# Six moves in the program of a two-block network: two waits of merge, x turned earlier, a gate batch and a gate placed elsewhere, the first norm's squares folded

## The chip, the cores and the metric

The kernel runs on one core of one Trainium2 chip, in one launch. The metric is the device time of a launch in microseconds. The core's engines each run their own program in order: TensorE (PE, matrix products into PSUM), VectorE (DVE), ScalarE (ACT), GpSimd (POOL), and SyncE (SP), which here only issues DMAs. They wait for one another by semaphores.

## The reference, cut to what matters

The network has 256 tokens and 1024 features, all in fp32. First block:

```
x += short_conv_mixer(rmsnorm(x));  x += conv_ffn(rmsnorm(x))
x += moba_attention(rmsnorm(x));    x += conv_ffn(rmsnorm(x));  x = rmsnorm(x)
```

Second block (`x = second_block(x)`), where `hybrid_mixer` has three branches, each under a gate, and `peer_ffn` picks 16 of 16384 experts per head and token:

```
def rmsnorm(x, g):        return x * rsqrt(mean(x*x, -1) + 1e-6) * g
def stick_breaking(q,k,v): z = q@k.T*scale; a = exp(logsig(z) + sum_behind(logsig(-z))); return a @ v
m = sig(g0)*(o_stick @ w_sb) + sig(g1)*(o_nsa @ w_nsa) + sig(g2)*(o_hgrn @ w_hgrn)
x = x + m @ w_out
peer: y = sum_e gate_e(token) * gelu(x @ u_e) * v_e      # gates from a top-k over sub-keys
x = x + y;  return rmsnorm(x)
```

## The kernel before, in words

**Layout.** Activations lie transposed: features on the 128 partitions, 256 tokens on the free axis; x is 8 tiles of 128x256. All weights come as one stream of chunks of 128x1024 (512 KB). A chunk goes through a ring of three slots: SyncE loads it (`stream_all`, L404), ScalarE rounds it to its high part (`split_hi`, L417), VectorE takes the rest as its low part (`split_lo`, L429), and TensorE multiplies. `exact` (L455 to L457) makes three products of every fp32 one: high by high, high by low, low by high. A chunk is thus 24 rows of 256 columns on TensorE, or 12 of 512 in the expert stage. `arrived` makes TensorE wait for the low part. `walk_act` and `walk_dve` are the splits of the chunk three places on, which ScalarE does once TensorE has finished the chunk that had the slot.

**Order.** It is written by hand: the block at the end of the kernel calls for each engine the stages one after the other, and helpers put the splits between a stage's own operations. Nothing is scheduled by a program. An instruction that waits holds back all that follows on its engine.

**The start** (`start_act`, `start_dve`, `gated_pe`). SyncE issues the parameter table (`par`, 128x356), the first chunk, x in two halves, and then the stream. TensorE multiplies the unnormed x (times its gains, split by L603 and L609), and the norm's factor is applied to the results. For the factor ScalarE squares x (L614), TensorE sums the squares over partitions with a matrix of ones (`sums_pe`, L545: 8 fp32 products, two records each), ScalarE takes the root (`root_act`, L618), VectorE the reciprocal (`recip_dve`, L643). `sc` is the first mixer: three input chunks per step, and from the third step on one output chunk. `fold_dve` adds 8 tiles of squares to 2, and is used in a later norm (`split_pe`).

**Joints.** Between stages `joint_act` and `joint_dve` add the result to x pair by pair of tiles (`residual_add_dve`, L695, as `pair_done` comes), split and square it, and TensorE sums the squares between the rows of the next chunk (`first_pe`, L545).

**Stick-breaking** (`stick_pe`, `stick_act`, `stick_dve`). Eight heads in phases: scores, sums behind (L1210 and L1211, a bank each for even and odd heads), values (L1219 to L1221). Of the 24 chunks of merge gates (`gate_pe`, `gate_act` L1191) the first eight are put between them. VectorE makes the log weights (L1301), and splits gate 6 after that of head 3.

**Merge** (`merge_pe`, `merge_act`, `merge_dve`). The 20 chunks of `BR`: 12 of the three branches, in banks 4 to 7 in turn, and 8 of the output product, (3, 0) to (3, 7). The gates go through a sigmoid (L1580) on ScalarE once all 24 are copied.

**The experts** (`peer_pe`, `peer_act`, `peer_dve`). 128 chunks up and 128 down. The map of gates is made in 32 batches of 8 tokens for each half of the experts: VectorE makes one-hot rows (L1884 to L1891, `hots`), TensorE multiplies them (L1910, 16 rows), VectorE applies the result to the experts' outputs (`take_gates`, L1900). ScalarE (L1970) and VectorE (L2009) split a gated output, and TensorE adds it into banks 0 to 3 (`down_tokens`, L506) on top of x, which `x_tokens_pe` (L497) has turned there by products with the identity. The batches of the second half run beside experts 0 to 63 down, two experts and a batch a step; expert 64 needs the last batch.

## Time and profile before

| | us |
|---|---|
| median of 3 runs | 1833.99 |
| the three runs | 1830.77, 1833.99, 1834.78 |
| profiled execution, its time | 1833.53 |
| its span | 1831.7 |
| TensorE busy (matmul) | 1782.5 (97%) |
| VectorE busy | 1377.0 (75%) |
| ScalarE busy | 874.6 (48%) |
| mean granted TensorE clock | 0.987 of full |
| DMA queue of SyncE, share of 16 engines | 47.1% |

The busy shares are means over very different stages. What a moved instruction is worth is read where it stands: in the timeline, which merges like instructions and says in brackets how long the engine was idle before them and who ended it. The chain that ended last is 81% TensorE, 14% VectorE, 3% ScalarE.

### The profile page before, as it was taken

To read this page: it belongs to the slowest core of one execution; us is meant where nothing else is said; L and a number is where in the kernel's file an instruction comes from. 1 tells how busy PE (TensorE), PEld (TensorE's weight loads), DVE (VectorE), ACT (ScalarE), POOL (GpSimd) and SP (SyncE) were. 2 spreads that over 40 slices of the span, in tenths; PEclk is the share of its full clock that TensorE was granted. 3 is DMA by queue.
4 is the path that set the end of the run, shared out by engine and by line. 5 is a ranking of instruction groups with operands and counts; after the bars stand their busy time and mean duration, and the time that the engine had idled before them with its cause. 6 is when DMAs were issued, how large, how long until landed. Compare 5 with 4: busy or idle time off the path is not lost.

```text
span 1831.7 us, 37775 instructions
## 1 busy us (share of the span) xinstructions
PE 1782.5 (97%) x13634; PEld 1674.5 (91%) x13634; DVE 1377.0 (75%) x2489; ACT 874.6 (48%) x1348; POOL 19.6 (1%) x40
## 2 busy tenths in 40 slices
PE   8999999999999999999999999999999999999998
PEld 8999999988999999988899999999999888878886
DVE  5788889855888877355767699977777689985665
ACT  4343335355343374565563645454444344444544
POOL 0000000010000000000100000000000000000000
PEclk9999999999999999899999999999999999999999
DMA  5545555432555546332235345554544455455553
GB/s 201 194 153 191 172 186 170 161 104 73 188 176 179 187 159 221 105 104 70 69 128 173 123 165 172 170 185 162 168 165 171 142 170 182 167 165 188 192 194 137
DMA packets 79997, 292.31 MB, mean 160 GB/s; under 512 B 8928, under 2 KB 9088, under 8 KB 79664
## 3 DMA queue, kind: packets, MB, share of 16 engines
q1 hardware_dynamic: 79200, 287.93, 47.1%
q0 software_dynamic: 720, 3.32, 0.5%
q8 instruction: 53, 0.87, 0.2%
q14 instruction: 24, 0.20, 0.0%
HBM read 290.16 MB, written 1.05 MB: 159 GB/s over the span
## 4 chain that ended last, share of the span: by engine, by line
PE 81%; DVE 14%; ACT 3%; issue 1%; DMA 1%; DVEq 0%; SPq 0%; ACTq 0%
PE ps L506 19%; PE ps L455 18%; PE ps L456 17%; PE ps L457 17%; DVE m L429 5%; PE ps L1910 2%; DVE m L1813 2%; DVE m L1809 1%; PE ps L461 1%; PE ps L545 1%; DVE m L1817 1%; PE ps L1070 1%; PE ps L1069 1%; ACT m L417 1%; ACT m L603 1%
## 5 line engine op out<-in xcount | busy, mean ns | idle before, releaser
L455 PE MATMUL ps<-m,m 128*128 128x256 f32 x3312 | 958.9, 290 | 23.0 <-DVE m L429 11.2
L456 PE MATMUL ps<-m,m 128*128 128x256 f32 x3312 | 941.5, 284 | 0.0
L457 PE MATMUL ps<-m,m 128*128 128x256 f32 x3312 | 941.0, 284 | 0.0
L429 DVE TENSOR_TENSOR m<-m,m 128x1024 fp32r<-128x1024 f32 x542 | 657.1, 1222 | 257.7 <-ACT m L417 250.8
L455 PEld LDWEIGHTS ps<-m,m 128*128 128x128 f32 x3312 | 638.8, 193 | 37.9 <-issue 24.4
L417 ACT ACTIVATE m<-m 128x1024 fp32r<-128x1024 f32 x542 | 565.4, 1050 | 170.4 <-PE ps L457 155.5
L456 PEld LDWEIGHTS ps<-m,m 128*128 128x128 f32 x3312 | 638.7, 193 | 1.2 <-issue 0.2
L457 PEld LDWEIGHTS ps<-m,m 128*128 128x128 f32 x3312 | 638.1, 193 | 0.0
L506 PE MATMUL ps<-m,m 128*128 128x512 f32 x1536 | 358.8, 393 | 2.0 <-DVE m L2009 2.0
L506 PEld LDWEIGHTS ps<-m,m 128*128 128x128 f32 x1536 | 287.0, 189 | 60.6 <-issue 2.1
L1970 ACT ACTIVATE m<-m 128x256 fp32r (+1 forms) x128 | 53.4, 418 | 202.6 <-PE ps L506 194.8
L1952 ACT ACTIVATE m<-ps 128x256 f32 (+1 forms) x128 | 49.4, 386 | 195.8 <-PE ps L457 195.7
L873 ACT ACTIVATE m<-m 128x256 f32<-128x256 f32 x44 | 18.4, 419 | 163.8 <-DVE m L830 163.8
L2009 DVE TENSOR_TENSOR m<-m,m 128x256 fp32r<-128x256 f32 x128 | 54.4, 426 | 52.0 <-ACT m L1970 50.4
L1891 DVE TENSOR_TENSOR m<-m,m 128x512 f16<-128x512 f16 x128 | 54.0, 422 | 7.5
L1900 DVE SCALAR_TENSOR_TENSOR m<-ps,m 128x512 f32 (+1 forms) x64 | 43.7, 683 | 2.2 <-PE ps L1910 2.2
L1887 DVE TENSOR_TENSOR m<-m,m 128x1024 f16<-128x1024 f16 x64 | 43.8, 685 | 0.0
L1910 PEld LDWEIGHTS ps<-m,m 128*128 128x128 f16 x1024 | 34.5, 97 | 9.7 <-issue 8.4
L828 DVE SCALAR_TENSOR_TENSOR m<-m,m,m 128x255 f32<-128x255 f32 x96 | 42.3, 478 | 0.3
L830 DVE SCALAR_TENSOR_TENSOR m<-m,m,m 128x254 f32<-128x254 f32 x96 | 42.2, 477 | 0.3
L1126 ACT ACTIVATE m<-m,m 128x128 f32<-128x128 f32 x64 | 28.5, 447 | 29.0 <-DVE m L1147 18.5
L1910 PE MATMUL ps<-m,m 128*128 128x64 f16 x1024 | 42.1, 194 | 0.0
(252 smaller groups left out, 1142.6 us busy)
## 6 DMA issues: line engine op xcount, KB each, us to landing
m<-stream SPq DMA_DIRECT2D x542, 512.0 KB, 3.3
m<-alibi_t POOLq DMA_DIRECT2D x1, 1536.0 KB, 11.4
m<-con SPq DMA_DIRECT2D x1, 1417.0 KB, 7.4
m<-xT SPq DMA_DIRECT2D x2, 512.0 KB, 8.2
y<-m SPq DMA_DIRECT2D x4, 256.0 KB, 2.6
m<-wcmpk POOLq DMA_DIRECT2D x1, 512.0 KB, 5.3
m<-wcmpv POOLq DMA_DIRECT2D x1, 512.0 KB, 5.5
m<-fin POOLq DMA_DIRECT2D x1, 512.0 KB, 4.3
```

The costliest lines, as they stand in the source:

```text
L417: nc.scalar.activation(w_hi[:, r, :], raw[:, r, :], ACT.Copy).then_inc(hi_done, 1)
L429: nc.vector.tensor_tensor(w_lo[:, r, :], raw[:, r, :], w_hi[:, r, :].bitcast(F32), ALU.subtract)\
L455: nc.tensor.matmul(out, lhs[0], rhs[0], start=start, stop=False, **kw)
L456: nc.tensor.matmul(out, lhs[0], rhs[1], start=False, stop=False, **kw)
L457: return nc.tensor.matmul(out, lhs[1], rhs[0], start=False, stop=stop, **kw)
L506: ins = nc.tensor.matmul(acc[:, 2 * c + h, :], lhs, rhs[:, slot, h * 512:h * 512 + 512], start=False, stop=last, skip_group_check=True)
L1887: nc.vector.tensor_tensor(hot_b, iota_b.unsqueeze(1).broadcast_to(sb_), pairs(idx[:, 1, tok]).broadcast_to(sb_), ALU.is_equal)
L1891: ins = nc.vector.tensor_tensor(hot_a[:, i], hot_a[:, 1], pairs(gate_part[:, i, tok]).broadcast_to(sa), ALU.mult)
L1910: ins = nc.tensor.matmul(out, hot_b[:, q // 2, :, q % 2], hot_a[:, i, q // 2, :, q % 2], start=i == 0, stop=i == 1)
L1952: nc.scalar.activation(emap[:, st.lin(1), :], ps[:, 4 + st.mod(2), 0:T], ACT.Gelu).then_inc(gelu_done, 1)
L1970: nc.scalar.activation(ez[st.mod(2)][0], emap[:, st.lin(1), :], ACT.Copy).then_inc(ez_hi, 1)
L2009: nc.vector.tensor_tensor(ez[p][1], emap[:, st.lin(a, b), :], ez[p][0].bitcast(F32), ALU.subtract)\
```

## The change

Six edits, independent of one another.

1. *Start.* The parameter table is loaded in two pieces: its first 8 columns by ScalarE, the rest by SyncE behind the second chunk of the stream. x comes in one DMA behind the first chunk; both engines wait for all of it. VectorE folds the squares to two tiles, and TensorE sums these (4 rows) after the third chunk of the mixer, where 16 rows stood after the second. The root goes behind the third `walk_act` of the first step, the reciprocal behind its third `walk_dve`.
2. *Stick.* Gate 6 follows the sixth sum behind, not the fourth.
3. *Merge's first wait.* The first two branch chunks do not wait for the 24th gate's copy.
4. *Merge's last wait.* VectorE does not wait for the last two output chunks.
5. *x turned.* The products with the identity stand ahead of the wait for the first gated expert.
6. *Last gate batch.* It stands between experts 62 and 63, and not behind 63. The loop over steps is one turn shorter, and its five last steps are written out.

```diff
@@ stream_all
+            if st.s == 1:
+                sp.dma_start(tabs[:, KD:NPAR], par[:, KD:NPAR]).then_inc(s_par, 16)
@@
+    def folded_pe(v, b):
+        for j in range(2):
+            ins = nc.tensor.matmul(ps[:, b, 0:T], ones[:, 0:P], v[:, j, :], start=j == 0, stop=j == 1)
+        ins.then_inc(sum_ready, 1)
@@ gated_pe
-                    if i == 0 and st.s == 0 and u == 1:
-                        for k in range(4):
-                            sums_pe(pe, 0, k)
+                    if i == 0 and st.s == 0 and u == 2:
+                        pe.wait_ge(sq_folded, 1)
+                        folded_pe(sq, 7)
@@ start_act
+        act.dma_start(tabs[:, 0:KD], par[:, 0:KD]).then_inc(s_gain, 16)
         split_hi(act, Step(0), 1, 0)
-        act.wait_ge(s_par, 16)
+        act.wait_ge(s_gain, 16)
+        act.wait_ge(s_x, 16)
         for k in range(4):
-            act.wait_ge(s_x[k // 2], 16)
             wide_hi_act(act, 0, k)
...
         split_hi(act, Step(2), 1, 0)
-        root_act(act, 0)
@@ start_dve
         split_lo(dve, Step(1), 1, 0)
+        dve.wait_ge(sq_part, 4)
+        fold_dve(dc, sq)
         split_lo(dve, Step(2), 1, 0)
+        dve.wait_ge(s_par, 16)
+
+    def first_factor_dve(dve, dc):
         recip_dve(dve, dc, 0)
         dc.link(nc.vector.tensor_tensor(rope_a, rstd, rstd, ALU.mult))
@@ sc_dve
-                if u == 1:
+                if st.s == 0 and u == 2:
+                    first_factor_dve(dve, dc)
+                if u == (2 if st.s == 0 else 1):
                     dve.wait_ge(c_copied, st.lin(1, 1))
@@ sc_act
             walk_act(act, st, *up_at("sc", 4, st.s, 2))
+            if st.s == 0:
+                root_act(act, 0)
@@ stick_pe
             sums_behind(j)
-            if j == 3:
+            if j == 5:
                 gate_pe(pe, 6)
@@ merge_pe
-            pe.wait_ge(gate_raw, 3 * KD)
+            if b >= 2:
+                pe.wait_ge(gate_raw, 3 * KD)
@@ merge_dve
-            if i == 3:
+            if i == 3 and m + 2 < KD:
                 dve.wait_ge(chunk_done, CH["br"] + e + 1)
-                if m + 2 < KD:
-                    merged_dve(dve, dc, m + 2)
+                merged_dve(dve, dc, m + 2)
@@ expert_down_pe
-        pe.wait_ge(z_ready, st.lin(a, b + ZB["peer"] + 1))
         n = a * st.s + b
         if n == 0:
             x_tokens_pe(pe)
+        pe.wait_ge(z_ready, st.lin(a, b + ZB["peer"] + 1))
@@ peer_pe
-        steps(pe, None, 0, NB, 6, third, first=2)
+        steps(pe, None, 0, NB - 1, 6, third, first=2)
+        expert_down_pe(pe, Step(HALF - 2), 1, 0)
+        gates_of_batch_pe(pe, 1, Step(NB - 1))
+        expert_down_pe(pe, Step(HALF - 1), 1, 0)
         steps(pe, None, HALF, NKEY - 1, 6, lambda st: expert_down_pe(pe, st, 1, 0))
@@ sync
-            sp.dma_start(tabs[:, :], par).then_inc(s_par, 16)
             sp.dma_start(raw[:, 0, :], stream[0, :, :]).then_inc(ring_full[0], 16)
-            for h in range(2):
-                sp.dma_start(x[:, 4 * h:4 * h + 4, :], xT[:, 4 * h:4 * h + 4, :]).then_inc(s_x[h], 16)
+            sp.dma_start(x[:, :, :], xT).then_inc(s_x, 16)
```

The later users of `sq_folded` in `split_pe` count one higher, as the start now uses it too.

VectorE at the start, in the kernel before. `m_2_51` is the low part of a chunk, `m_14_63` the reciprocal root, `m_19_68` its square, `m_20_69` and `m_18_67` the scaled products.

```order
L429 TENSOR_TENSOR m_2_51<-m_0_49,m_1_50 128x1024 [waits chunk_hi_ready] x2
L643 RECIPROCAL m_14_63<-m_13_62 128x256 [waits rms_ready]
L676 TENSOR_TENSOR m_19_68<-m_14_63 128x256 [waits dve_chain]
L429 TENSOR_TENSOR m_2_51<-m_0_49,m_1_50 128x1024 [waits chunk_hi_ready,dve_chain]
L429 TENSOR_TENSOR m_2_51<-m_0_49,m_1_50 128x1024 [waits chunk_hi_ready]
L892 TENSOR_TENSOR m_20_69<-m_21_70,m_19_68 128x256 [waits c_copied]
L893 TENSOR_TENSOR m_18_67<-ps,m_14_63 128x256
L429 TENSOR_TENSOR m_2_51<-m_0_49,m_1_50 128x1024 [waits chunk_hi_ready,dve_chain]
```

The same place in the changed kernel, where `m_42_91` are the squares.

```order
L432 TENSOR_TENSOR m_2_51<-m_0_49,m_1_50 128x1024 [waits chunk_hi_ready]
L713 TENSOR_TENSOR m_42_91<-m_42_91 128x1024 [waits square_ready]
L714 TENSOR_TENSOR m_42_91<-m_42_91 128x512 [waits dve_chain]
L432 TENSOR_TENSOR m_2_51<-m_0_49,m_1_50 128x1024 [waits chunk_hi_ready]
L432 TENSOR_TENSOR m_2_51<-m_0_49,m_1_50 128x1024 [waits chunk_hi_ready,params_loaded]
L432 TENSOR_TENSOR m_2_51<-m_0_49,m_1_50 128x1024 [waits chunk_hi_ready] x2
L651 RECIPROCAL m_14_63<-m_13_62 128x256 [waits rms_ready]
L689 TENSOR_TENSOR m_19_68<-m_14_63 128x256 [waits dve_chain]
L902 TENSOR_TENSOR m_20_69<-m_21_70,m_19_68 128x256 [waits c_copied,dve_chain]
L903 TENSOR_TENSOR m_18_67<-ps,m_14_63 128x256
```

The two folding sums have come in behind the second chunk's split, and the splits of the fourth to sixth chunk stand ahead of the reciprocal, where two stood behind it and one behind the scaled products.

TensorE in the stick stage, before. `m_57_106` are the heads' log terms, `m_4_53` and `m_5_54` the two parts of the activations, `m_1_50` and `m_2_51` those of the chunk.

```order
L1210 MATMUL ps<-m_57_106,m_15_64 128x384 [waits log_weight_ready,softplus_whole]
L1211 MATMUL ps<-m_57_106,m_9_58 128x128
L455 MATMUL ps<-m_4_53,m_1_50 128x256 [waits chunk_lo_ready0,merge_gate_copied]
L456 MATMUL ps<-m_5_54,m_1_50 128x256
L457 MATMUL ps<-m_4_53,m_2_51 128x256
```

And in the changed kernel.

```order
L1222 MATMUL ps<-m_57_106,m_15_64 128x384 [waits log_weight_ready,softplus_whole]
L1223 MATMUL ps<-m_57_106,m_9_58 128x128
L1222 MATMUL ps<-m_57_106,m_15_64 128x384 [waits log_weight_ready,softplus_whole]
L1223 MATMUL ps<-m_57_106,m_9_58 128x128
L1222 MATMUL ps<-m_57_106,m_15_64 128x384 [waits log_weight_ready,softplus_whole]
L1223 MATMUL ps<-m_57_106,m_9_58 128x128
L458 MATMUL ps<-m_4_53,m_1_50 128x256 [waits chunk_lo_ready0,merge_gate_copied]
L459 MATMUL ps<-m_5_54,m_1_50 128x256
```

Two more pairs of sums, heads 4 and 5, stand between head 3's and the gate.

TensorE in the step of experts 62 and 63, before. `m_6_55`, `m_7_56` and `m_95_144`, `m_96_145` are the two parts of even and odd gated experts, `m_94_143` and `m_93_142` the one-hot rows.

```order
L506 MATMUL ps<-m_1_50,m_95_144 128x512 [waits chunk_lo_ready0]
L506 MATMUL ps<-m_1_50,m_95_144 128x512
L506 MATMUL ps<-m_2_51,m_95_144 128x512 x2
L506 MATMUL ps<-m_1_50,m_96_145 128x512 x2
L506 MATMUL ps<-m_1_50,m_95_144 128x512 x2
L506 MATMUL ps<-m_2_51,m_95_144 128x512 x2
L506 MATMUL ps<-m_1_50,m_96_145 128x512 x2
L1904 REGISTER_ALU
L1910 MATMUL ps<-m_94_143,m_93_142 128x64 [waits gate_map_taken,one_hots_ready]
L1910 MATMUL ps<-m_94_143,m_93_142 128x64 x15
```

And in the changed kernel.

```order
L509 MATMUL ps<-m_1_50,m_6_55 128x512 x2
L509 MATMUL ps<-m_2_51,m_6_55 128x512 x2
L509 MATMUL ps<-m_1_50,m_7_56 128x512 x2
L1922 MATMUL ps<-m_94_143,m_93_142 128x64 [waits gate_map_taken,one_hots_ready]
L1922 MATMUL ps<-m_94_143,m_93_142 128x64 x15
L509 MATMUL ps<-m_1_50,m_95_144 128x512 [waits chunk_lo_ready0,z_ready]
L509 MATMUL ps<-m_1_50,m_95_144 128x512
```

The 16 rows of the batch now stand behind the even expert's rows and ahead of the odd one's.

## Rows read from the trace of the kernel before

**Rows 1.** The page, busy us, share of the span, instructions.

```profile
PE 1782.5 (97%) x13634; PEld 1674.5 (91%) x13634; DVE 1377.0 (75%) x2489; ACT 874.6 (48%) x1348; POOL 19.6 (1%) x40
```

**Rows 2.** Chain of waits, start: start us, us, what.

```profile
1.67 7.78 DMA m<-xT
...
12.39 0.21 PE ps L457
...
19.07 0.12 PE ps L455
```

**Rows 3.** The instructions that load x: their landings.

```profile
DMA to landing us min/median/max: 7.8/8.2/8.6
```

**Rows 4.** Timeline of the start: start us, us, instructions, idle before.

```profile
11.62 0.55 PE L455 MATMUL ps<-m,m 128*128 128x256 f32 x1 [4.21 <-DVE m L609]
...
19.63 3.61 PE L545 MATMUL ps<-m,m 128*128 128x256 f32 x16
...
23.79 1.75 DVE L643 RECIPROCAL m<-m 128x256 f32<-128x256 f32 x1 [5.71 <-ACT m L618]
...
27.31 0.39 PE L455 MATMUL ps<-m,m 128*128 128x256 f32 x1 [1.20 <-DVE m L429]
...
33.24 2.44 DVE L429 TENSOR_TENSOR m<-m,m 128x1024 fp32r<-128x1024 f32 x2
```

**Rows 5.** VectorE, lines of `fold_dve`, 640 to 700 us.

```profile
L700 DVE TENSOR_TENSOR m<-m 128x1024 f32<-128x1024 f32 x2 | 2.4, 1218 | 0.0
...
L701 DVE TENSOR_TENSOR m<-m 128x512 f32<-128x512 f32 x2 | 1.4, 692 | 0.1
```

**Rows 6.** Windows: length; busy PE, PEld, DVE, ACT, POOL; granted clock; DMA share, GB/s.

```profile
699.30:706.00 6.70, 6.70 (x33) 6.70 (x33) 5.86 (x4) 0.55 (x3) 0.00 (x0) 0.50 1.00 344
...
818.80:822.10 3.30, 3.30 (x15) 3.00 (x14) 0.00 (x0) 0.48 (x1) 0.00 (x0) 0.50 0.28 103
...
945.00:948.40 3.40, 3.40 (x19) 3.40 (x17) 2.83 (x3) 3.37 (x3) 0.00 (x0) 0.50 0.16 28
...
1006.50:1009.80 3.30, 2.90 (x9) 2.58 (x10) 3.30 (x8) 3.30 (x9) 0.00 (x0) 0.50 0.30 114
```

**Rows 7.** Timeline, stick stage.

```profile
817.17 0.36 PE L455 MATMUL ps<-m,m 128*128 128x256 f32 x1 [2.36 <-DVE m L429]
...
828.21 0.41 PE L1219 MATMUL ps<-m,m 128*128 128x64 f32 x2 [0.79 <-DVE m L1512]
```

**Rows 8.** Timeline, last gate and first branch chunks of merge.

```profile
944.54 0.38 PE L455 MATMUL ps<-m,m 128*128 128x256 f32 x1 [2.82 <-ACT m L1191]
...
945.45 1.28 ACT L1580 ACT_TABLE_LOAD   x1
...
946.74 1.91 ACT L1580 ACTIVATE m<-m 128x2048 f32<-128x2048 f32 x1
...
950.39 1.22 DVE L429 TENSOR_TENSOR m<-m,m 128x1024 fp32r<-128x1024 f32 x1
...
963.38 1.22 DVE L429 TENSOR_TENSOR m<-m,m 128x1024 fp32r<-128x1024 f32 x1
```

**Rows 9.** Timeline, end of merge; last row: the first joint.

```profile
1003.47 1.23 DVE L429 TENSOR_TENSOR m<-m,m 128x1024 fp32r<-128x1024 f32 x1 [5.06 <-PE ps L457]
...
1006.90 2.05 PE L545 MATMUL ps<-m,m 128*128 128x256 f32 x4 [3.52 <-ACT m L614]
...
111.25 1.10 PE L545 MATMUL ps<-m,m 128*128 128x256 f32 x4 [0.18 <-ACT m L614]
```

**Rows 10.** Timeline, before the first expert down.

```profile
1446.35 5.47 PE L497 MATMUL ps<-m,m 128*128 128x128 f32 x32 [3.69 <-DVE m L2009]
```

**Rows 11.** Timeline, around the last gate batch.

```profile
1639.03 5.71 PE L506 MATMUL ps<-m,m 128*128 128x512 f32 x24
...
1640.46 0.88 DVE L1891 TENSOR_TENSOR m<-m,m 128x512 f16<-128x512 f16 x2
...
1647.19 9.18 PE L506 MATMUL ps<-m,m 128*128 128x512 f32 x32 [1.95 <-DVE m L2009]
```

More of the change, by code:

```diff
@@ L313, in build @@
     y_sum, y_mean, y_r = (at(O_HH + 3 * D + 8 * i, 2) for i in range(3))
-    s_x = sem("x_first_half_loaded"), sem("x_second_half_loaded")
+    s_x = sem("x_loaded")
+    s_gain = sem("first_weights_loaded")
     s_par = sem("params_loaded")
@@ L664, in start_act @@
         split_hi(act, Step(2), 1, 0)
-        root_act(act, 0)
     def start_dve(dve, dc):
         split_lo(dve, Step(0), 1, 0)
-        dve.wait_ge(s_par, 16)
+        dve.wait_ge(s_gain, 16)
+        dve.wait_ge(s_x, 16)
         for k in range(4):
-            dve.wait_ge(s_x[k // 2], 16)
             wide_lo_dve(dve, 0, k)
         split_lo(dve, Step(1), 1, 0)
+        dve.wait_ge(sq_part, 4)
+        fold_dve(dc, sq)
         split_lo(dve, Step(2), 1, 0)
+        dve.wait_ge(s_par, 16)
+    def first_factor_dve(dve, dc):
         recip_dve(dve, dc, 0)
@@ L704, in split_pe @@
         g, c = TC["p_split"], CH["p_split"]
-        def folded(v, b):
-            for j in range(2):
-                ins = nc.tensor.matmul(ps[:, b, 0:T], ones[:, 0:P], v[:, j, :], start=j == 0, stop=j == 1)
-            ins.then_inc(sum_ready, 1)
         for n in range(16):
@@ L720, in split_pe @@
             if n == 3:
-                pe.wait_ge(sq_folded, 1)
-                folded(sq, 7)
+                pe.wait_ge(sq_folded, 2)
+                folded_pe(sq, 7)
             if n == 6:
-                pe.wait_ge(sq_folded, 2)
-                folded(sq2, 5)
+                pe.wait_ge(sq_folded, 3)
+                folded_pe(sq2, 5)
         gates_pe(pe)
```

## The prediction, made before the result was known

> **What bounds the kernel now.** I began with the page: TensorE is busy for 1782.5 of the 1831.7 us [rows 1]. The profiled execution took 1833.53 us, so 1.8 us lie outside its span. Nothing but TensorE time can pay, and there are two kinds of it: its 49 us of pauses, and its rows at the lower of its two clock levels. I then went through TensorE's timeline for every row that has an idle time in front of it, and through the windows for the granted clock. At 0.50 (1.2 GHz) a row of 256 columns follows the last by 0.21 us, at 1.00 (2.4 GHz) by 0.12 us [rows 2]. So 3.4 us at the lower level hold work for 1.9 us, and cost 1.5. It is also lower in three places that the diff does not touch; the longest, 6.7 us at 699, stands for them [rows 6]. Its lower stretches at 818.8, 945.0 and 1006.5 [rows 6] each begin within 1.7 us of a pause of 2.4 to 3.5 us, and all three pauses are ones that the diff touches [rows 7 to 9]. So are the pauses of 3.69 us at 1446.35 and of 1.95 us at 1647.19 [rows 10, 11]. The change is therefore worth what these five stretches and the start are worth, each read by itself.
>
> **The start.** Before: x is issued at 1.67 us, its first half lands 7.78 us later, the second at most 8.6 us after its own issue [rows 2, 3], so at 10.7. From the first landing to the first weight row at 11.62 are 2.2 us of ScalarE and VectorE. Now the parameter table (178 KB) no longer stands ahead of the weights and x, and both engines wait for all of x. The table's place is worth between 0 and 1.1 us: x whole lands between 9.6 and 10.7. I take 9.9 (the queue had data to move in all of the time it would save, but the engines did not move it evenly), so the first weight row comes at 12.0, 0.4 later, and costs 0.2 us net because that time is at the lower clock. The small DMA of eight columns of the table, now issued by ScalarE, hides in the 7 us before x.
> The sums of squares: 16 rows in 3.47 us (19.63 until 23.1) become 4 rows, 0.87 us; this saves 2.6 us [rows 4]. VectorE pays for it with a fold of 1.22 + 0.69 us [rows 5]. It falls where VectorE idles before the third chunk's low part. Squares end near 16.3, the fold at 18.2, the low part at 19.4; TensorE, without the sums, wants that chunk at 19.8. Covered, with 0.3 us to spare.
> The pause of 1.20 us at 27.31 ends on VectorE's split of the fourth chunk [rows 4], which stood behind the root and the reciprocal (1.75 us at 23.79). Now the three splits go ahead of the reciprocal, and the pause goes. But something is late next. ScalarE comes to the root's table load only after the sixth chunk's high part (23.8); the load is 1.28 us [rows 8], so the root runs at 25.1, the reciprocal at 25.6, 1.85 us later than before. Without the three splits, which took 3.5 us of VectorE, the seventh chunk's split moves from 33.24 [rows 4] to 33.24 + 1.85 - 3.5 = 31.6 and ends at 32.85. TensorE, 3.6 us ahead, wants it at 32.2: a new pause of about 0.7 us. Net: 2.6 + 1.2 - 0.2 - 0.7 = 2.9 us. Bounds: 1.0 (x at 10.7 and the fold not covered), 4.5 (the clock rises earlier and the pause stays out).
> The table load was followed by its activation 0.01 us after its end, at 946.74 [rows 8]. The Trainium skill (ScalarE: Activation LUTs, section What ACT_TABLE_LOAD costs) gives such a switch some 1.4 us more, for a drain. By that the start would be worth 1.5 us and not 2.9; the trace disagrees.
>
> **The stick gate.** TensorE has done four sums when it stands 2.36 us before gate 6, until 817.17 [rows 7]: VectorE splits that gate's low part only after the fourth log weight. With two more sums (0.93 us each, by the spacing of the four) ahead of the gate, TensorE stands from 816.5 to 817.15. The gate then runs at the higher clock, sums 6 and 7 follow without a pause, since their log weights are made during the gate. Values 0 and 1 end at 823.2. Value 2 waits, as it does now for 0.79 us, for VectorE: the last log weight, one split of 1.22 us, one copy, and starts at 824.2 and not at 828.21 [rows 7]. Gain 4.0 us: 2.5 of pauses and 1.5 of clock. Bounds 2.2 and 4.4. Behind it stand the window heads, whose pace TensorE sets; nothing falls due there by the clock on the wall.
>
> **Merge's first wait.** TensorE pauses for 2.82 us at 944.54 for ScalarE's copy of the last gate [rows 8]. Chunks 0 and 1 of the merge no longer wait for it: both are split (the second's low part at 940.7), their banks, 4 and 5, are free. They run from 941.7 at the higher clock until 947.5. Chunk 2 keeps the wait, passed at 944.5. Then VectorE is next: it is occupied from 945.53 on, and its split of chunk 3 runs at 950.39 [rows 8] behind products that do not come from TensorE. It ends at 951.6; TensorE wants it at 950.35: a pause of 1.3 us. The eighth chunk's split, at 963.38 [rows 8], moves by no more than 0.7 us: in between VectorE follows ScalarE's three sigmoids of 1.9 us (the first at 946.74) and the high parts between them, which lose only a wait of 0.6 us on TensorE. It ends at 963.9. Before, TensorE came to the eighth chunk at 944.54 + 7 x 24 x 0.12 + 1.5 = 966.2; now at 964.0. Gain 2.2 us, where the wait and the clock alone would give 4.3. Bounds 0.8 and 4.3.
>
> **Merge's last wait.** VectorE stands for 5.06 us until the end of merge (1003.47), does one split, two residual adds, and only then can ScalarE square; TensorE stands for 3.52 us [rows 9]. Without the wait VectorE adds pair by pair while the last chunk runs, which is what it does at the first joint, where TensorE's pause is 0.18 us at 111.25 [rows 9]. Of the lower clock from 1006.5 to 1009.8 [rows 6] TensorE works through 2.9 us, which cost 1.4. Gain 3.34 + 1.4 = 4.8 us. Bounds 3.3 and 4.9.
>
> **x turned first.** The 32 rows that put x under the experts start at 1446.35 after 3.69 us and take 5.47 us [rows 10], 3.4 us of it at the lower clock, so 3.8 us at the higher. Now they start at 1442.66 and end at 1446.45, just after the first gated row is ready (1446.3). The experts start there and not at 1451.6: gain 5.1 us. Low bound 3.7, the pause alone.
> The clock came back to its higher level at 1450.2 while TensorE had run nothing but these turning rows since 1446.35. The Trainium skill (TensorE: Matmul & The Clock Gate, section Part 4: PE-mode transpose) says that transposes do not count as busy for the clock. By that rule the turns would not hold it, and the gain would be 3.7; the trace disagrees, if it holds for turns written as plain matmuls.
>
> **The last gate batch.** Experts 62 and 63 take 5.71 us from 1639.03; the batch follows, VectorE applies it, ScalarE and VectorE split expert 64, and TensorE stands 1.95 us [rows 11]. The 32 rows behind it take 9.18 us, against 7.61 at the pace of the 24 before: 1.57 us of clock. Now the batch stands between 62 and 63, at 1641.9; its one-hot rows are made by 1641.34 [rows 11]. VectorE's application ends near 1643.8, the split of 64 at 1644.9, and expert 63 runs until 1645.3. Gain 3.5 us. Low bound 1.5, if the one-hot rows come late or the clock falls anyway. The loop loses one turn and six steps stand written out (89 rows more in TensorE's program); straight code elsewhere shows no pause of its own, so I cost it at nothing.
>
> **The sum.** 2.9 + 4.0 + 2.2 + 4.8 + 5.1 + 3.5 = 22.5 us. 1833.5 - 22.5 = 1811.0. The profiled execution was 0.46 us below the median of 1833.99, so I forecast a median of 1811.5 us.
>
> **Rivals.**
> A. The pauses go and the clock falls all the same (or falls in other places, because the later stages stand elsewhere against its changes, as the 6.7 us at 699 may do). For it: small pauses of 0.7 to 1.3 us stay in three of the places. Against: the pause of 0.79 us at 828.21 [rows 7] and that of 1.20 us at 27.31 have no fall behind them. Price 5 x 1.5 = 7.5 us: 1819.0. One part of it is that the turning rows do not hold the clock, by itself 1.4 us: 1812.9, with 0.04 of the chance. It is what the Trainium skill (TensorE: Matmul & The Clock Gate, section Part 4: PE-mode transpose) would have; the trace disagrees. Chance of all of A 0.15.
> B. VectorE and ScalarE become the bound in more places than I see, above all at the start, in stick and in merge. Half of these three terms is 4.5 us: 1816.0. For it: in merge it is so already, and takes 2.1 us of the term. Against: VectorE is busy for 75% of the span only. Chance 0.13.
> C. Slower than before. The six written-out steps of the third expert loop are read at the pace of instruction supply. The piece from 62 back is 6 steps of 6.0 us. It decides once they take more than 22.5 + 3.7 us longer together, 4.4 us per step; at twice their time it is +36 - 22.5: 1847.5. Against: rows in the straight parts of the program follow one another at 0.12 us. Chance 0.02, with 0.02 more for a landing of x that slips by several microseconds on top of A.
> D. Merge's last wait is not what holds the residual adds, because the split ahead of them (which waits for ScalarE's high part) takes its place; then 3.3 of 4.8 us are missing and the time is 1814.8. Against: that high part is made at 997.7. Chance 0.04.
>
> **Numbers.** The forecast has 0.64, with its own range of 1807.5 to 1815.5. The three runs of before spread over 4.0 us, so the range needs 2 us at either side of any sum. The low end adds the upper bounds of the start, stick and merge (1.6 + 0.4 + 2.1, not all at once): 1806. The high end takes in B and A: 1820. The measurement can tell about 0.2% (3.7 us) from nothing: faster 0.95, within 0.02, slower 0.03.
>
> **What would show it.** Right: no idle time above 1.0 us in front of TensorE's rows at the stick gate, in the first joint behind merge and before experts 0 and 64; a granted clock of 1.00 at those four; 4 rows of sums at the start; merge's first branch directly behind the last gate, and a new pause of about 1.3 us before its fourth chunk; one of 0.7 us near 32. Wrong: the pauses gone and stretches at 0.50 still there (A), new waits on the split by VectorE longer than 1.5 us (B), idle time of kind "issue" in the written-out steps (C).

## The result, and the profile after

The change made the kernel faster. The median of four runs is 1808.05 us (1807.17 to 1808.78), against 1832.72 us (1830.77 to 1834.78) for the kernel before; the ratio is 0.9865, with a 95% interval of 0.9848 to 0.9882. Forecast were 1811.5 us and a range of 1806 to 1820.

The profiled execution took 1808.72 us, its span is 1806.9 us, the mean granted clock 0.993 (before 0.987). From the page, TensorE's line (busy us, share of the span, instructions), which answers to [rows 1]:

```profile
PE 1771.0 (98%) x13622; PEld 1664.1 (92%) x13622; DVE 1378.8 (76%) x2491; ACT 874.4 (48%) x1348; POOL 19.5 (1%) x40
```

The twelve instructions fewer are the folded sums. TensorE's busy time fell by 11.5 us. Those twelve rows, at the 0.22 us that one took before [rows 4], are 2.6 us of it; the rest is work at the higher clock.

The start, from the timeline of each engine (start, duration, line, instructions; in brackets the idle time in front and what ended it). It answers to [rows 4, 5]; lines 455, 609, 643, 700 and 701 of before are 458, 617, 651, 713 and 714 here, and further down 497, 506, 545, 1219 and 1910 are 500, 509, 548, 1231 and 1922; the folded sums have a line of their own, 565:

```profile
7.55 3.30 ACT L611 ACTIVATE m<-m,m 128x256 fp32r<-128x256 f32 x8 [2.34 <-DMA m<-xT]
...
13.92 1.23 DVE L713 TENSOR_TENSOR m<-m 128x1024 f32<-128x1024 f32 x1 [0.85 <-ACT m L622]
15.18 0.69 DVE L714 TENSOR_TENSOR m<-m 128x512 f32<-128x512 f32 x1
15.79 3.48 DVE L432 TENSOR_TENSOR m<-m,m 128x1024 fp32r<-128x1024 f32 x3
...
9.63 0.36 PE L458 MATMUL ps<-m,m 128*128 128x256 f32 x1 [2.59 <-DVE m L617]
...
17.06 0.39 PE L458 MATMUL ps<-m,m 128*128 128x256 f32 x1 [0.81 <-DVE m L432]
...
20.04 1.02 PE L565 MATMUL ps<-m,m 128*128 128x256 f32 x4
...
30.89 0.36 PE L458 MATMUL ps<-m,m 128*128 128x256 f32 x1 [1.20 <-DVE m L432]
```

x is whole at 7.5 us; the first weight row comes at 9.63 and not at 11.62. The fold stands in front of VectorE's next split, and TensorE waits for that split for 0.81 us at 17.06. The sums are 4 rows. The pause that was expected near 32 is there too, at 30.89.

The other five places on TensorE, the first joint last; it answers to [rows 7 to 11]. The query of the row at 1621.31 ends at 1632 us, and its 47 instructions are those up to there:

```profile
809.62 0.36 PE L458 MATMUL ps<-m,m 128*128 128x256 f32 x1 [0.50 <-DVE m L432]
...
816.53 0.41 PE L1231 MATMUL ps<-m,m 128*128 128x64 f32 x2 [0.79 <-DVE m L1524]
...
941.57 0.36 PE L458 MATMUL ps<-m,m 128*128 128x256 f32 x1 [1.59 <-DVE m L432]
...
953.40 0.36 PE L458 MATMUL ps<-m,m 128*128 128x256 f32 x1 [0.32 <-DVE m L432]
...
990.94 1.10 PE L548 MATMUL ps<-m,m 128*128 128x256 f32 x4 [0.17 <-ACT m L622]
...
1096.45 0.36 PE L458 MATMUL ps<-m,m 128*128 128x256 f32 x1 [1.94 <-DVE m L432]
...
1426.63 3.81 PE L500 MATMUL ps<-m,m 128*128 128x128 f32 x32
...
1620.82 0.66 PE L1922 MATMUL ps<-m,m 128*128 128x64 f16 x16
1621.31 10.92 PE L509 MATMUL ps<-m,m 128*128 128x512 f32 x47
...
106.16 1.10 PE L548 MATMUL ps<-m,m 128*128 128x256 f32 x4 [0.18 <-ACT m L622]
```

The 2.36 us at the stick gate are 0.50, the 3.52 us behind merge 0.17, and before experts 0 and 64 there is no idle time. The 1.94 us at 1096.45 stood in the kernel before as well (at 1113.81); no edit touches them.

The windows (columns as in [rows 6]): three stretches at the lower clock, then the turning of x, expert 64, the stick gate and the joint behind merge:

```profile
695.10:698.50 3.40, 3.40 (x19) 3.40 (x18) 3.40 (x3) 0.00 (x0) 0.00 (x0) 0.50 1.02 366
...
818.00:821.40 3.40, 3.40 (x18) 3.40 (x18) 1.42 (x2) 0.00 (x0) 0.00 (x0) 0.50 0.46 165
...
1097.90:1101.30 3.40, 3.40 (x18) 3.40 (x18) 3.40 (x4) 0.39 (x2) 0.00 (x0) 0.50 0.80 283
...
1426.60:1430.20 3.60, 3.60 (x39) 3.60 (x35) 2.07 (x4) 1.71 (x4) 0.55 (x1) 1.00 0.83 267
1624.00:1630.00 6.00, 6.00 (x28) 4.98 (x27) 4.43 (x5) 2.94 (x6) 0.00 (x0) 1.00 0.51 167
...
809.60:813.00 3.40, 3.38 (x26) 3.27 (x27) 1.93 (x3) 2.95 (x7) 0.00 (x0) 1.00 0.56 176
990.90:994.30 3.40, 3.36 (x21) 3.19 (x22) 3.10 (x8) 3.40 (x9) 1.29 (x3) 1.00 0.07 19
```

The clock held at the start, at the stick gate, at merge, at the turning and at expert 64. It fell at 818.0, 1.5 us behind the start of value 2, and, newly, at 1097.9. Added up over the recorded trace and without the last 8 us, TensorE was at the lower level for 41.0 us before (twelve times 3.4) and for 20.5 us after (six times). At 1.5 us lost for each 3.4, that is 9 of the 24.8 us by which the span shrank; the other 15.8 us are pauses and rows. These 9 us hold for the two profiled executions; other executions of the same kernels had other clocks (see the last section).

Where the 24.8 us came from, as differences between the same instructions in the two traces, against the terms of the prediction. The last column is the part that the lower clock has in the difference, at 1.5 us for each 3.4:

| stretch, and between which instructions | forecast | traces | of it clock |
|---|---|---|---|
| start, to the first joint's sums (111.25, 106.16) | 2.9 | 5.1 | about 2 |
| to stick's gate 6 (817.17, 809.62): a pause of 0.4 near 136, the stretch at 699 halved | 0 | 2.5 | 1.6 |
| stick, gate 6 to value 2 | 4.0 | 4.1 | 1.5 |
| the same, the fall at 818.0 behind it | 0 | -1.5 | -1.5 |
| merge up to its end (last output row) | 2.2 | 2.4 | 1.5 |
| merge's last wait (to the routing, 1035.92, 1018.56) | 4.8 | 4.75 | 1.4 |
| the fall at 1097.9, behind the routing's pause | 0 | -1.5 | -1.5 |
| x turned first | 5.1 | 5.2 | 1.5 |
| last gate batch, to the last row | 3.5 | 3.7 | 1.6 |

### The profile page after: what moved, and what is told of

Same layout as the page of the kernel before. It is cut to its first block, busy times and chain, and to the rows that moved or that the text cites. A ratio compares the mean times of both kernels' runs of the same rounds, so it can differ in the third digit from the quotient of the medians.

```text
span 1806.9 us, 37729 instructions
## 1 busy us (share of the span) xinstructions
PE 1771.0 (98%) x13622; PEld 1664.1 (92%) x13622; DVE 1378.8 (76%) x2491; ACT 874.4 (48%) x1348; POOL 19.5 (1%) x40
## 4 chain that ended last, share of the span: by engine, by line
PE 80%; DVE 13%; ACT 4%; issue 2%; DMA 1%; DVEq 0%; ACTq 0%; SPq 0%
PE ps L509 19%; PE ps L458 17%; PE ps L459 17%; PE ps L460 17%; DVE m L432 5%; PE ps L1922 2%; DVE m L1825 2%; DVE m L1821 1%; ACT m L420 1%; PE ps L464 1%; DVE m L1829 1%; PE ps L548 1%; PE ps L1082 1%; PE ps L1081 1%; DMA m<-stream 1%
```

## The experiments

Twelve kernels ran. Six hold one of the change's parts each and are the kernel before otherwise; the others change the kernel after. The median of the kernel before was 1832.61 us beside the first four, 1830.43 us beside the next four and 1829.88 us beside the last four. In a trace each edit is judged by its own stretch; the whole time carries the falls of the clock too. There is one trace of each kernel, so a fall that is there in one and missing in another can also be the difference between two executions.

### The start alone

The kernel after, the other five edits undone; of one of these the diff is:

```
             sums_behind(j)
-            if j == 5:
+            if j == 3:
```

> The kernel after with its other five edits undone: only the start's order of loads, its separate gain table, one landing of x and the folded squares are new. Main theory: the start is worth what it is worth between the two traces up to the 700th us, 7.3 us (5.1 until the first row of sums at 106 us, 0.5 at a pause near 136 us that goes, and 1.6 where the low-clock stretch near 699 us shortens from 6.8 to 3.4 us), so 1825.4 us at a median of 1832.7 before. Rival (the pattern of clock falls depends on the place of later stages and is repaid): the 1.6 us near 699 does not come and the time is 1827.1. Rival by the terms of the prediction: the start is worth 2.9 us, 1829.8. Granted clock 1.00 from the first weight row on in the first two cases.

Measured: 1823.6 us (1821.42 to 1828.67), ratio 0.9949 (0.9929 to 0.9969), 9.0 us by the medians. The first weight row comes at 9.42 and the first joint's sums at 105.83:

```profile
105.83 1.10 PE L548 MATMUL ps<-m,m 128*128 128x256 f32 x4 [0.18 <-ACT m L622]
...
715.00:718.40 3.40, 3.40 (x19) 3.40 (x18) 0.87 (x1) 0.21 (x1) 0.00 (x0) 0.51 0.83 283
```

That is 5.4 us earlier than before (111.25). So the start's term was too small in the prediction, by 2.2 to 2.5 us. The fall of 6.8 us at 699 is missing here. There is one of 3.4 us at 715, although the stage stands some 6 us earlier: that fall did not keep its place in the stage. Ahead of it stands a pause of 2.06 us (at 713.74), where the kernel before has one of 0.82 (at 721.25). The trace does not show the rest of the 9.0 us: it is of the slowest of the four executions, and its span is 4.8 us below that of the kernel before.

### What made x early: the table's place

```
-            sp.dma_start(raw[:, 0, :], stream[0, :, :])...
+            sp.dma_start(tabs[:, KD:NPAR], par[:, KD:NPAR]).then_inc(s_par, 16)
+            sp.dma_start(raw[:, 0, :], stream[0, :, :])...
```

> The kernel after, with the larger part of the parameter table (88 of its 89 groups of columns' worth of bytes) issued on SyncE's queue ahead of the first chunk and x, as in the kernel before, instead of behind the second chunk. Theory A (the table ahead holds the transfers back): x is whole about 1 us later (8.4 to 8.6 us against 7.5), the first weight row starts near 10.5 us instead of 9.6, and because rows then come after 9.7 us the clock falls at the start as it did before: 2 to 4 us slower than the kernel after (1810 to 1812). Theory B (the split of x in two transfers held x back, not the table): the first weight row stays within 0.3 us of 9.6 and the time within 0.5 us of 1808.0.

Measured: 1808.69 us (1807.51 to 1809.85), ratio 0.9873 (0.9854 to 0.9893). TensorE's timeline, and windows:

```profile
11.24 0.55 PE L456 MATMUL ps<-m,m 128*128 128x256 f32 x1 [3.59 <-DVE m L615]
```

```profile
4.00:6.50 2.50, 2.50 (x8) 1.96 (x7) 0.00 (x0) 0.88 (x1) 0.00 (x0) 1.00 0.73 278
...
10.20:17.00 6.80, 5.76 (x27) 5.79 (x28) 5.90 (x11) 6.50 (x13) 0.00 (x0) 0.50 0.41 157
818.00:821.40 3.40, 3.12 (x27) 3.15 (x28) 2.04 (x5) 1.51 (x2) 0.00 (x0) 1.00 0.47 154
1097.90:1101.30 3.40, 3.40 (x31) 3.40 (x30) 3.40 (x3) 1.31 (x2) 0.00 (x0) 1.00 0.83 273
```

The same window of the kernel after, and then of the kernel before, where the DMA engines move least:

```profile
4.00:6.50 2.50, 2.50 (x10) 2.04 (x9) 1.22 (x1) 1.06 (x1) 0.00 (x0) 1.00 0.95 383
```

```profile
4.00:6.50 2.50, 2.50 (x8) 2.00 (x7) 0.46 (x1) 1.06 (x1) 0.00 (x0) 1.00 0.59 155
```

The last columns are the DMA engines' share and GB/s. With the 174 KB of table ahead, the DMA engines move 278 GB/s between 4.0 and 6.5 us, without it 383 GB/s, and x is whole 1.6 us later (9.06 against 7.47 us). The table by its bytes would be 0.5 us. So theory A holds for the landing and for the first fall: the row comes 1.6 us later, the clock falls at 10.2, and at the first joint this kernel is 2.1 us behind. And yet the whole time is the same: the falls at 818 and at 1098 are absent. Their pauses are still there: stick's 0.50 and 0.79 us and the routing's 1.94 us are in this trace to 0.01 us. Theory A had 2 to 4 us for the whole and was wrong there.

### x in two halves

```
-            sp.dma_start(x[:, :, :], xT).then_inc(s_x, 16)
+            for h in range(2):
+                sp.dma_start(x[:, 4 * h:4 * h + 4, :], ...).then_inc(s_x[h], 16)
 ...                                     (and both engines wait for s_x[k // 2])
```

> The kernel after, with x loaded as two transfers of half its columns and each half waited for alone, as in the kernel before; the tables keep their new places. Theory B (two transfers of half rows hold x back): the second half is whole later than 7.5 us by 1 us or more, the first weight row later than 9.6, and the clock falls at the start: 1810 to 1812 us. Theory A (the table did it): the first half is there by about 6 us, the first weight row can start up to 1 us earlier than 9.6 (8.7 to 9.6), and the time is 1807.0 to 1808.3, the clock at 1.00 throughout the start.

Measured: 1804.95 us (1803.54 to 1807.02), ratio 0.9855 (0.9834 to 0.9875).

```profile
9.02 0.36 PE L458 MATMUL ps<-m,m 128*128 128x256 f32 x1 [1.12 <-DVE m L617]
```

The first half is there at 6.84 us, the second only at 8.41, 0.9 us later than x in one piece; the first row comes 0.6 us earlier. With the table's 1.6 us these 0.9 us make up 2.5 of the 3.2 us by which x was whole later in the kernel before; the last 0.7 us no run explains. Since the first half comes sooner, one landing for all of x cost 0.6 us of the change's start. Theory A was right on the first half and the row; of theory B the late second half is there (0.9 us), but the row did not wait for it and the clock did not fall. The median is 3.1 us below that of the kernel after, under either theory's range, and 2.5 us of that are not the start. The trace points to the clock: it has two stretches below 1.00 (3.4 us at 693.4, 6.8 us at 758.3) and none at 818 or 1098, and its span is 5.1 us shorter. In its window from 4.0 to 6.5 us the DMA engines move 253 GB/s, without a table ahead, so x in halves lowers their rate too.

### The fold undone

```
-                        pe.wait_ge(sq_folded, 1)
-                        folded_pe(sq, 7)
+                        for k in range(4):
+                            sums_pe(pe, 0, k)
 ...                                      (and no fold_dve in start_dve)
```

> The kernel after with the first norm's squares not folded: VectorE's two additions (1.23 and 0.69 us) go and TensorE multiplies eight tiles of squares by ones instead of two, at the same place. Main theory: TensorE does four rows more on its clock at 1.00, 0.11 to 0.12 us each, 6 more rows are 0.7 us, and the rest of the start is bound by TensorE, so about 0.7 us slower than after, 1808.7; VectorE's 1.9 us less moves the splits forward and can shorten the pauses of 0.81 us at 17.1 us and 1.20 us at 30.9 us. Rival (those pauses are what VectorE's fold costs): they shrink by more than 1 us together and the unfolded kernel is as fast or faster, 1806.8 to 1808.0.

Measured: 1807.71 us (1807.1 to 1808.76), no difference to the kernel after. My price for a row was wrong in the expectation: 12 instructions more, at 0.22 us as in [rows 4], are 2.6 us. From the first weight row (9.57) to the first joint it takes 97.5 us, against 96.5 us in the kernel after, with a fall of 3.4 us at 10.1 in it and without the pauses of 0.81 and 1.20 us:

```profile
107.06 1.10 PE L548 MATMUL ps<-m,m 128*128 128x256 f32 x4 [0.17 <-ACT m L622]
...
10.10:13.50 3.40, 3.40 (x19) 3.40 (x18) 2.89 (x6) 3.40 (x7) 0.00 (x0) 0.51 0.18 70
```

So the rival was right on the pauses, which are the fold's price, and the fold is worth at most 1 us, not 2.6. The fall begins ahead of the place of the fold and of the sums, and costs up to 1.5 us; if it is no part of the edit, the fold is worth nothing. The whole time is equal because the falls at 818 and 1098 are missing here too.

### Stick's gate alone

```
             sums_behind(j)
-            if j == 3:
+            if j == 5:
                 gate_pe(pe, 6)
```

> The kernel before with one edit: in the stick heads' stage, TensorE's gate 6 comes after the sixth tile of sums instead of after the fourth. Theory A (the wait of 2.36 us for VectorE's split is hidden, and with it the fall of the clock at 818.7 us, which cost 1.6 us): 4.0 us faster than before, 1828.6. Theory B (the fall of the clock goes with where the stage stands in time and not with that wait, since in the kernel after it fell there too): the wait shrinks by 1.9 us and 1.7 to 2.3 us is all, 1830.3 to 1831.0. Behind the stage every pause and every clock fall stays as before (945, 1006, 1447, 1648 us, each earlier by the gain) in theory A; in theory B up to one more or one fewer fall of 3.4 us at half clock is possible further on, each worth 1.5 to 1.7 us.

Measured: 1828.67 us (1824.58 to 1833.34, 10 runs), ratio 0.9993 (0.9981 to 1.0006): not told from no change. The stretch itself, and the windows of two falls:

```profile
815.93 0.35 PE L455 MATMUL ps<-m,m 128*128 128x256 f32 x1 [0.50 <-DVE m L429]
...
822.85 0.41 PE L1219 MATMUL ps<-m,m 128*128 128x64 f32 x2 [0.79 <-DVE m L1512]
```

```profile
824.10:827.50 3.40, 3.40 (x18) 3.40 (x18) 1.42 (x2) 0.00 (x0) 0.00 (x0) 0.51 0.44 131
940.10:946.90 6.80, 6.19 (x29) 6.19 (x30) 4.94 (x5) 5.36 (x6) 0.00 (x0) 0.50 0.23 77
```

From gate 6 to value 2 it takes 6.92 us, against 11.04 us: 4.1 us less, the forecast's term. But the fall that was at 818.7 is at 824.1, 1.3 us behind the start of value 2, and the one at merge is twice as long (6.8 us at 940.1). That is theory B for the clock: the fall did not go with the wait. The stretch's 4.1 us are shown by the trace; in the whole time they are not. The medians differ by 1.8 us, and the interval includes no change at all.

### Merge's last wait alone

```
-            if i == 3:
+            if i == 3 and m + 2 < KD:
                 dve.wait_ge(chunk_done, CH["br"] + e + 1)
-                if m + 2 < KD:
-                    merged_dve(dve, dc, m + 2)
+                merged_dve(dve, dc, m + 2)
```

> The kernel before with one edit: in the merge, VectorE no longer waits for the last two output chunks ahead of the next stage's work, as its wait for them is gone where it has nothing to write. Prediction's term: the idle time of 3.52 us of TensorE in front of the first row of sums of the next norm shrinks to about 0.2 us and the clock fall at 1006.4 us (1.5 us) goes: 4.8 us faster than before, 1827.9. Rival: the idle time goes and the clock falls all the same in this stage or the next, 3.3 us, 1829.4.

Measured: 1823.74 us (1821.72 to 1826.95, 10 runs), ratio 0.9960 (0.9948 to 0.9972), 6.7 us.

```profile
997.20 1.10 PE L545 MATMUL ps<-m,m 128*128 128x256 f32 x4 [0.18 <-ACT m L614]
```

From the end of merge to the routing it takes 27.8 us, against 32.5: 4.7 us, as forecast. The clock did not fall here. Nor did it at the stick gate (814.09) and at merge's first wait (939.92), whose pauses of 2.37 and 2.83 us are as they were. The span of this trace is 10.3 us below that of the kernel before; 4.7 of it are this stretch, and most of the rest is clock (27.3 us at the lower level against 41.0).

### The turning alone

```
-        pe.wait_ge(z_ready, st.lin(a, b + ZB["peer"] + 1))
         n = a * st.s + b
         if n == 0:
             x_tokens_pe(pe)
+        pe.wait_ge(z_ready, st.lin(a, b + ZB["peer"] + 1))
```

> The kernel before with one edit: TensorE turns the 16 tiles of x for the first expert's output ahead of its wait for ScalarE's gated row, not behind it. Prediction's term: the turning (2.8 to 3.6 us at half clock with the fall at 1446.8 us) moves into the idle time of 3.69 us, so 5.1 us (3.7 if the clock falls all the same), 1827.6. Rival: the turning rows do not count as work that holds the clock up, the clock falls at the wait all the same, 3.7 us and 1829.0; granted clock 0.50 in the first 3.4 us behind the turning shows it.

Measured: 1825.14 us (1818.86 to 1827.44, 10 runs), ratio 0.9965 (0.9950 to 0.9981), 5.3 us.

TensorE's timeline, up to 1443 us:

```profile
1438.18 3.81 PE L497 MATMUL ps<-m,m 128*128 128x128 f32 x32
1442.02 1.21 PE L506 MATMUL ps<-m,m 128*128 128x512 f32 x4
```

From the end of the work in front to the first expert's row it takes 3.8 us, against 8.9: 5.1 us. The rival falls: with the turning rows in the pause the clock stayed at 1.00 behind them, here and in the seven other kernels that have this edit. In the six traces in which the 3.69 us stood idle it fell each time.

### The pause before value 2 filled

```
         for j in range(n):
+            if j == 2:
+                keep_clock_pe(6, 3)
             values(j)
```

> The kernel after with one addition: six rows of ones on ones into an unused bank of PSUM, in front of TensorE's wait of 0.79 us for VectorE's copy at 816.5 us, just ahead of the stretch at half clock of 818.0 us. They change nothing of the result's numbers and lie in the idle time (6 rows of 0.11 us are 0.66 us). Theory A (this pause makes the clock fall): no fall at 818 us, 1.5 us faster than the kernel after, 1806.5. Theory B (falls in this stage go with the stage's place in time, and with the whole stretch of short rows in it): the clock falls at 818 us again or the fall moves, and the time is 1808.0 within 0.5.

Measured: 1807.65 us (1807.43 to 1809.42), as the kernel after. TensorE's timeline and windows:

```profile
814.13 2.81 PE L543 MATMUL ps<-m 128*128 128x256 f32 x12
816.78 0.33 PE L1231 MATMUL ps<-m,m 128*128 128x64 f32 x2
```

```profile
818.00:821.40 3.40, 3.40 (x32) 3.40 (x30) 1.42 (x2) 0.16 (x1) 0.00 (x0) 1.00 0.17 29
```

The six rows are twelve instructions of 0.22 us: they fill 2.65 us where 0.79 were to be had, and cost 1.7 us. The clock did not fall at 818; but neither did it with the table first, with x in halves and with the fold undone, where the pause is as it was. The run doesn't tell whether the fill did it. The falls at 1096.5 and, newly, at 11.0 are in its trace.

### Merge's first wait alone

```
-            pe.wait_ge(gate_raw, 3 * KD)
+            if b >= 2:
+                pe.wait_ge(gate_raw, 3 * KD)
```

> The kernel before with one edit: in the merge, TensorE's first two chunks do not wait for ScalarE's last copy of a gate, only the third one does. Prediction's term: 2.2 us faster than before, of which the idle time of 2.82 us at 944.54 us is the source; what is left of it is one pause of 1.3 to 1.6 us ahead of the fourth chunk. Rival (nothing is saved, since the fourth chunk and the later ones wait for the same splits of ScalarE and VectorE as before): under 0.8 us. A clock fall more or less elsewhere moves the whole time by up to 1.7 us beyond either.

Measured: 1825.79 us (1824.12 to 1829.1, 10 runs), ratio 0.9982 (0.9971 to 0.9993), 4.1 us.

```profile
944.71 0.36 PE L455 MATMUL ps<-m,m 128*128 128x256 f32 x1 [1.59 <-DVE m L429]
...
997.43 1.92 PE L545 MATMUL ps<-m,m 128*128 128x256 f32 x4 [3.52 <-ACT m L614]
```

From the first product at L1696, ahead of merge, to merge's last row it takes 107.5 us, against 109.9: 2.4 us. Of the 2.82 us 1.59 are back ahead of the fourth chunk, and the fall at 945 is gone.

### The last gate batch alone

```
-        steps(pe, None, 0, NB, 6, third, first=2)
+        steps(pe, None, 0, NB - 1, 6, third, first=2)
+        expert_down_pe(pe, Step(HALF - 2), 1, 0)
+        gates_of_batch_pe(pe, 1, Step(NB - 1))
+        expert_down_pe(pe, Step(HALF - 1), 1, 0)
```

> The kernel before with one edit: the last batch of one-hot gate products comes one expert earlier in TensorE's order, between the output chunks of experts 62 and 63, so that VectorE and ScalarE have an expert's length to make the gated row that expert 64 waits for. Prediction's term: the idle time of 1.95 us at 1647.2 us goes, and with it the clock fall at 1648.1 us, 3.5 us faster than before. Rival: the same wait of about 2 us appears ahead of another expert, or the clock falls all the same at another pause: 0 to 2.0 us.

Measured: 1825.92 us (1823.39 to 1828.81, 10 runs), ratio 0.9978 (0.9966 to 0.9990), 4.0 us.

TensorE's timeline, up to 1650 us:

```profile
1640.80 0.66 PE L1910 MATMUL ps<-m,m 128*128 128x64 f16 x16
1641.30 8.88 PE L506 MATMUL ps<-m,m 128*128 128x512 f32 x38
```

No idle time between the batch and the experts behind it. From the first expert's row to the last row: 367.5 us, against 371.2, 3.8 us.

### Three more splits moved

With x in halves, and:

```
-            nc.scalar.activation(v, v, ACT.Sigmoid).then_inc(sg_ready, 1)
             walk_act(act, Step(e), 1, CH["br"])
+            nc.scalar.activation(v, v, ACT.Sigmoid).then_inc(sg_ready, 1)
...
         gate_dve(dve, 23)
+        walk_dve(dve, Step(0), 1, CH["br"])
...
                     first_factor_dve(dve, dc)
+                    walk_dve(dve, Step(1), *up_at("sc", 4, 1, 0))
...
-        yield 0.6
+        yield 1.2
...
-            yield 2.2
+            yield 2.2 - 0.6 * c
```

> A version meant to beat both: the kernel after, with x loaded in two halves each waited for alone (1804.95 alone), and three more moves of a split ahead of other work: in the merge ScalarE's and VectorE's split of the fourth chunk ahead of the first sigmoid and of the last head group's chain (idle time of 1.59 us at 941.6 us), in the first stage VectorE's split of the seventh chunk ahead of the chain of the first tile (1.20 us at 30.9 us), and in the expert routing VectorE's split ahead of the first addition of 128x2048 (1.94 us at 1096.5 us). If each idle time goes but 0.7 us: 1.6 + 1.2 + 1.2 = 4.0 us, so 1801.0. If the moves only shift the waits: 1804.0 to 1805.5. One fall of the clock more or fewer is 1.5 to 1.7 us.

Measured: 1805.63 us (1803.6 to 1810.56), ratio 0.9871 (0.9844 to 0.9899): no faster than x in halves alone (1804.95), and 4.6 us above the 1801.0 expected. TensorE at three places, then VectorE at the middle one:

```profile
29.20 0.39 PE L458 MATMUL ps<-m,m 128*128 128x256 f32 x1 [0.36 <-DVE m L909]
...
942.49 0.39 PE L458 MATMUL ps<-m,m 128*128 128x256 f32 x1 [2.30 <-DVE m L432]
...
1100.07 0.36 PE L458 MATMUL ps<-m,m 128*128 128x256 f32 x1 [0.29 <-DVE m L432]
```

```profile
939.67 0.69 DVE L1769 TENSOR_TENSOR m<-m,ps 128x512 f32<-128x512 f32 x1 [0.85 <-ACT m L1594]
940.39 0.69 DVE L1771 TENSOR_TENSOR m<-m,m 128x512 f32<-128x512 f32 x1
```

The 1.20 us at 30.9 became 0.36, the 1.94 us at 1096 became 0.29 (and 0.20 at 1136). But the merge's 1.59 us passed from the fourth chunk to the fifth and grew to 2.30: VectorE now waits 0.85 us at 939.67 for the second sigmoid, and its branch product stands ahead of the split. The clock fell at 942.7.

### Two of the three

> The same version without the move in the first stage. Against it that move is worth 1.2 us if the idle time at 30.9 us goes and nothing behind it becomes late: 1802.2 here. If VectorE's chain of the first tile, late by 1.2 us with the move, holds what follows, this kernel is as fast or faster, 1801.0.

Measured: 1807.89 us (1806.35 to 1808.81), ratio 0.9877 (0.9856 to 0.9899); 1802.2 was expected. The move in the first stage is worth 0.85 us of pause (the first tile's work on VectorE, made late by it, holds nothing that shows); 0.54 us more are a first row that came later here (9.33 against 8.79), for no edit. Next to that its trace has 3.4 us more at the lower clock (20.5 against 17.1).

## Why the prediction came out right

**The pauses.** Of the six terms five were within 0.2 us of what the traces give for the stretches: stick 4.1 (4.0), merge's first wait 2.4 (2.2), its last wait 4.75 (4.8), turning 5.2 (5.1), last batch 3.7 (3.5). Each edit alone gave the same figure in its own stretch, to 0.1 us. Every expected remainder was found: 0.50 us at the gate, 1.59 us ahead of merge's fourth chunk, nothing at experts 0 and 64.

**The mis-sized term: the start.** It was put at 2.9 and is 5.1 us, beyond its upper bound of 4.5. The step that failed is "I take 9.9": x was whole at 7.5 us. The prediction let the table cost no more than 1.1 us and put the loading in halves at nothing. The table costs 1.6 us, as the run with the table first shows, and the halves another 0.9. The row that I expected 0.4 us later came 2.0 us earlier, and the clock did not fall behind it. "Covered, with 0.3 us to spare" failed as well: the fold cost a pause of 0.81 us, as TensorE, now at the higher clock, was there sooner. That VectorE would be late for the seventh chunk was right, with 1.20 us and not 0.7. The fold, which I put at 2.6 us, is worth 1 us at most. So the start's term was too low although one of its parts was too high.

**Rival A, in part.** Behind four of the five pauses that the diff shortens the clock held; behind the stick stage it fell at 818.0, and at 1097.9 a fall is new, 1.5 us each. The stretch at 699 lost 3.4 of its 6.8 us, worth 1.6. The prediction had counted the clock as belonging to the pauses. What the start brought beyond its term (2.2), and the stretches before stick (2.5), less the two new falls (3.0) and with the small terms, is the 2.3 us by which the profiled execution is below 1811.0.

**Luck in the total.** That the total is so near is in part chance. The start and the stretches before stick brought 4.7 us that nobody had forecast, and the new falls took 3.0 back. The kernel before scatters as well: beside the experiments it ran 50 times with a median of 1830.2 us and a granted clock of 0.989, while the forecast starts from 1833.99 and the profiled execution had 0.987. Against these 50 runs the change is worth some 22 us and not 24.7. So the 2.5 us before stick, and a part of the 9 us of clock, may be the scatter of the kernel before and no work of the change; no second trace of it is there to tell.

**The others.** B: one half of it, in the start. C: the written-out steps ran without a pause; TensorE has no idle time above 0.25 us anywhere behind 1198 us. D: merge's last wait was what held the adds; alone it gave 4.7 us.

**What stays open.** The single edits add to 30.8 us by their medians and to 25.5 us by their stretches, the whole to 24.7. The medians of before in the three groups differ by 2.7 us and single runs spread over up to 10 us, so the first figure is not in conflict with the last. What decides where the clock falls between kernels with the same pauses was not found; nor why the DMA engines move less when the table goes first or x comes in halves.

## What to carry to other kernels

Price a pause by its own stretch, from the same instruction to the same instruction, and expect that. A fall of the clock may or may not come with it (here at each pause of 3.5 us or more, at some of those of 2 us), so judge an edit of a few microseconds by the stretch in the trace and the granted clock beside the median. When you move a split ahead on one engine, look at the other engine's work that its product waits for: the pause may only pass to the next chunk. At a kernel's start, put the part of a table that the first operation needs on another queue and the rest behind the first weights and inputs. Only the place of the rest was tested alone.

## What the hardware showed that I had not expected

The same program runs at different times with the clock alone: in 50 runs of the kernel before, those with a mean granted clock of 0.992 took 1827.4 us on average (6 runs), those with 0.989 took 1830.2 (8), and those with 0.986 took 1834.0 (11). Between 0.992 and 0.986 lie 22 us at the lower level, six stretches of 3.4 us more or fewer in one and the same program. The four runs of the kernel after stayed within 1.6 us, but those of the last kernel but one, with as few pauses, spread over 7.0.

A short pause does not settle whether the clock falls. With pauses of 0.50 and 0.79 us at stick and of 1.94 us in the routing, equal to 0.01 us, the clock fell behind them in the kernel after and not in the kernels with the table first, with x in halves or unfolded, which reached the first joint 2.1 us later, 0.7 us earlier and 0.9 us later.

The long pauses are another matter. Over the fourteen traces, counting a fall that begins within the pause or at most 1.7 us behind its end:

| pause of TensorE, where | us | traces that have it | with a fall |
|---|---|---|---|
| before the turning of x | 3.69 | 6 | 6 |
| behind merge | 3.52 | 6 | 6 |
| merge's first wait | 2.82 | 6 | 5 |
| stick gate | 2.36 | 6 | 3 |
| merge's fifth chunk, in the last two kernels | 2.30 | 2 | 2 |
| before expert 64 | 1.95 | 6 | 4 |
| routing | 1.94 | 12 | 3 |
| merge's fourth chunk | 1.59 | 6 | 0 |

So the clock's share that the prediction counted behind merge and before the experts is borne out by every trace. At the stick gate and before expert 64 it depends on the execution. Falls also come without a pause: each of the fourteen traces has one or more between 693 and 771 us, and before the one at 699.2 in the kernel before TensorE does not stand still.

174 KB of a table with 1392 bytes for each partition, issued ahead, delayed 1 MB behind it by 1.6 us (9.06 against 7.47 us), over three times what its bytes take at 383 GB/s.
